# Ten-stage transformer kernel: stage ends with y weighed before its root, x ended by one operation, squares of x by halves, one weight split on GpSimd, modulation between Rwkv's turns

## What is computed

```python
x = x + 0.5 * rmsnorm(swiglu(rmsnorm(x, ng[0]), ...), ng[1])        # feed-forward
h = rmsnorm_2(x, norm_w[i, 0]) * (1.0 + sc1) + sh1                  # mixers of the second block
y = short_conv_mixer(h, ...)
x = x + gt1 * rmsnorm_2(y, norm_w[i, 1])
def rmsnorm(x, g, eps=NORM_EPS):
    y = xf * lax.rsqrt(jnp.mean(xf * xf, -1, keepdims=True) + eps)
    return y * g
```

## Time and profile before

| | us |
|---|---|
| three runs | 3035.13, 3039.06, 3039.35 |
| profiled execution | 3035.5 |
| its span | 3033.6 |
| TensorE matmuls busy | 2805.1 (92%) |
| VectorE busy | 1293.2 (43%) |
| ScalarE busy | 1121.9 (37%) |
| GpSimd busy | 162.3 (5%) |
| mean granted TensorE clock | 0.962 |
| read from HBM | 697.5 MB, 230 GB/s over the span |

### The profile page before, as it was taken

One profiled execution on the slowest core, in us unless ns is written; L12 is line 12 of the kernel. 1 busy time (PEld: TensorE's weight loads), 2 busy tenths in 40 slices (PEclk: granted clock), 3 DMA queues, 4 the chain that ended last, 5 costly groups with the idle time before them and its releaser, 6 DMA issues.

```text
span 3033.6 us, 44027 instructions
## 1 busy us (share of the span) xinstructions
PE 2805.1 (92%) x18364; PEld 2211.1 (73%) x18364; DVE 1293.2 (43%) x2125; ACT 1121.9 (37%) x2008; POOL 162.3 (5%) x146
## 2 busy tenths in 40 slices
PE   8989879999989999799899999999896879999998
PEld 6879657887878888578797666666695856666665
DVE  5546267546557544364563121212474551121212
ACT  5444245435457222254443222222454251222222
POOL 0000000000000222100010000000003300000000
PEclk9999899999999999799999999999897989999999
DMA  8524657436434111065244899999550036999996
GB/s 338 184 104 167 250 224 303 181 139 236 181 139 168 42 56 56 28 234 193 107 174 174 361 415 415 417 414 416 217 180 1 1 125 276 417 415 416 413 418 252
DMA packets 96401, 701.53 MB, mean 231 GB/s; under 512 B 10688, under 2 KB 10816, under 8 KB 11328
## 3 DMA queue, kind: packets, MB, share of 16 engines
q1 hardware_dynamic: 96192, 698.59, 58.0%
HBM read 697.50 MB, written 1.05 MB: 230 GB/s over the span
## 4 chain that ended last, share of the span: by engine, by line
PE 86%; DVE 6%; ACT 4%; issue 2%; DMA 1%; POOL 1%; SPq 0%; DVEq 0%; ACTq 0%
PE bank L1576 15%; PE bank L811 11%; PE bank L813 11%; PE bank L812 11%; PE bank L1636 8%; PE bank L1554 4%; PE bank L1663 4%; PE bank L1914 2%; PE bank L1922 2%; PE bank L1926 2%; DMA weight_ring<-weight_slots 1%; DVE h_sb L716 1%; PE bank L2429 1%; PE bank L1445 1%; PE bank L1448 1%
## 5 line engine op out<-in xcount | busy, mean ns | idle before, releaser
L1576 PE MATMUL bank<-weight_ring,packed_h 128*64 128x256 f32 x2176 | 285.4, 379 | 0.0
L811 PE MATMUL bank<-source_hi_lo,weight_hi_lo 128*128 128x256 f32 x864 | 252.3, 292 | 14.8 <-DVE source_hi_lo L801 11.7
L1576 PE MATMUL bank<-more_slots,packed_h 128*64 128x256 f32 x1920 | 257.0, 379 | 1.5 <-ACT packed_h L1563 1.5
L811 PE MATMUL bank<-gate_up_hi_lo,x_hi_lo 128*128 128x512 f32 x640 | 253.4, 396 | 1.4 <-DVE gate_up_hi_lo L929 1.4
L1576 PEld LDWEIGHTS bank<-weight_ring,packed_h 128*64 128x64 f32 x2176 | 196.6, 137 | 74.0 <-issue 18.1
L813 PE MATMUL bank<-gate_up_hi_lo,x_hi_lo 128*128 128x512 f32 x640 | 249.8, 390 | 0.0
L812 PE MATMUL bank<-gate_up_hi_lo,x_hi_lo 128*128 128x512 f32 x640 | 249.2, 389 | 0.0
L812 PE MATMUL bank<-source_hi_lo,weight_hi_lo 128*128 128x256 f32 x864 | 249.0, 288 | 0.0
L813 PE MATMUL bank<-source_hi_lo,weight_hi_lo 128*128 128x256 f32 x864 | 248.7, 288 | 0.0
L1576 PEld LDWEIGHTS bank<-more_slots,packed_h 128*64 128x64 f32 x1920 | 174.3, 137 | 69.4 <-issue 15.4
L770 DVE TENSOR_TENSOR weight_hi_lo<-weight_ring,weight_hi_lo 128x1024 fp32r<-128x1024 f32 x138 | 168.2, 1221 | 100.6 <-ACT weight_hi_lo L764 100.6
(11 more groups left out here) (548 smaller groups left out, 5409.6 us busy)
## 6 DMA issues: line engine op xcount, KB each, us to landing
weight_ring<-weight_slots SPq DMA_DIRECT2D x443, 1024.0 KB, 7.4
more_slots<-weight_slots SPq DMA_DIRECT2D x212, 1024.0 KB, 9.0
params_sb<-small_params SPq DMA_DIRECT2D x1, 3196.5 KB, 17.7
h_sb<-weight_slots SPq DMA_DIRECT2D x3, 1024.0 KB, 5.8
y_sb<-weight_slots SPq DMA_DIRECT2D x3, 1024.0 KB, 7.9
x_sb<-x_by_tokens SPq DMA_DIRECT2D x1, 1024.0 KB, 4.8
out_by_tokens<-x_sb SPq DMA_DIRECT2D x4, 256.0 KB, 2.2
params_sb<-small_params SPq DMA_DIRECT2D x1, 69.5 KB, 4.6
```

The costliest lines, as they stand in the source:

```text
L811: e.matmul(out, w[0], x[0], start=start, stop=False, skip_group_check=shared)
L1576: mm = e.matmul(ps[x * CAP:(x + 1) * CAP, m * FB:(m + 1) * FB], self.hc[:, c, (2 * (p % 2) + x) * CAP:(2 * (p % 2) + x + 1) * CAP], wt[:, ...
```

## The change

1. In `back_dve` VectorE multiplies y by the gain row (`out_weighed`) as soon as a bank's square is made, ahead of the reciprocal. One operation then ends x: y_tok times the inverse root, plus x.
2. Of x's norm, the squares of q=1 are made in halves of 512 features, each as soon as its half of x is new; VectorE turns the first sum into a bias (`x_part`). VectorE scales all of x, four operations of 512 columns; ScalarE scales none. The head of VectorE comes wholly behind the stage's last operation on x.
3. In NsaSsd, Conv and Delta GpSimd makes the low part of split 0 alone; split 1 is made by ScalarE and VectorE behind the sources. A slot is free when both its units' low parts are made (`done` with two signals).
4. In Rwkv the first of the four modulation steps stands between the turns of q=0 and q=1 on TensorE, and VectorE makes the low part of split 0 behind `norm_dve`'s first part.

```diff
@@ head_act
-        for q in range(TT):
-            self.squares_act(e, q)
-            e.wait_ge(*k.ge("x_inverse", n, q))
-            e.activation(k.h_tok[:, q, 0:512], k.x[:, q, 0:512], ACT.Copy, scale=k.x_inv[:, q:q + 1])
-            if q == 0:
-                self.begin(e)
-                self.first_split_act(e)
+        self.squares_act(e, 0)
+        for f in range(2):
+            cut = slice(f * 512, f * 512 + 512)
+            e.wait_ge(*k.ge(*self.x_key(1, f)))
+            e.activation(k.y_tok[:, 1, cut], k.x[:, 1, cut], ACT.Square, accum_out=k.x_sums[:, 1 + f:2 + f])
+        e.wait_ge(*k.ge("x_half_squared", n, 1))
+        e.wait_ge(*k.ge("x_part", n))
+        e.activation(k.x_dev[:, 1:2], k.x_sums[:, 2:3], ACT.Sqrt, scale=1.0 / D, bias=k.x_part[:, 0:1])
+        self.begin(e)
+        self.first_split_act(e)
@@ head_dve
-        self.scaled_dve_half(e, 1)
+        self.inverse_of_x_dve(e, 0)
+        self.scale_x_dve(e, 0, 0)
+        e.wait_ge(*k.ge("x_half_squared", n, 0))
+        e.tensor_scalar(k.x_part[:, 0:1], k.x_sums[:, 1:2], 1.0 / D, NORM_EPS, ALU.mult, ALU.add)
+        self.scale_x_dve(e, 0, 1)
+        self.inverse_of_x_dve(e, 1)
+        for f in range(2):
+            self.scale_x_dve(e, 1, f)
@@ back_dve
         for q in range(TT):
-            e.wait_ge(*k.ge("out_squared", n, 2 * q))
-            e.tensor_scalar(k.y_part[:, q:q + 1], ...)
+            for f in range(2):
+                b, cut = 2 * q + f, slice(f * 512, f * 512 + 512)
+                if q == 0:
+                    e.wait_ge(*gain_in(f))
+                e.wait_ge(*k.ge("out_squared", n, b))
+                if f == 0:
+                    e.tensor_scalar(k.y_part[:, q:q + 1], ...)
+                e.tensor_tensor(k.y_tok[:, q, cut], k.bank[b][:, :], self.gain_row[:, cut], ALU.mult)
             e.wait_ge(*k.ge("out_deviation", n, q))
             e.reciprocal(k.y_inv[:, q:q + 1], k.y_dev[:, q:q + 1])
             e.wait_ge(*k.ge("out_inverse", n, q))
             for f in range(2):
-                e.scalar_tensor_tensor(out=k.y_tok[:, q, cut], in0=k.bank[2 * q + f][:, :], scalar=k.y_inv[:, q:q + 1], in1=self.gain_row[:, cut], ...)
-            if nxt and q:
-                nxt.first_half_dve(e)
-            for f in range(2):
-                e.tensor_tensor(k.x[:, q, cut], k.x[:, q, cut], k.y_tok[:, q, cut], ALU.add)
+                e.scalar_tensor_tensor(out=k.x[:, q, cut], in0=k.y_tok[:, q, cut], scalar=k.y_inv[:, q:q + 1], in1=k.x[:, q, cut],
+                                       op0=ALU.mult, op1=ALU.add)
@@ plan_units
-            k.weights.done(i, self.lo_key(u))
+            k.weights.done(i, self.lo_key(u), self.lo_key(u - 1))
@@ Conv, NsaSsd, Delta
-        self.plan_units(12, column_half, 2)
+        self.plan_units(12, column_half, 1)
-        self.norm_act(e, ..., lambda: self.split_act(e, 1))
+        self.norm_act(e, ...)
+        self.split_act(e, 1)
         self.norm_dve(e, ...)
+        self.split_dve(e, 1)
-        self.split_pool(e, 1)
@@ Rwkv
-        self.norm_pe(e)
-        k.modulation.fill(e, "PE", 4)
+        self.norm_pe(e, lambda: k.modulation.fill(e, "PE", 1))
+        k.modulation.fill(e, "PE", 3)
-        self.split_dve(e, 0)
-        self.norm_dve(e, k.par("a1_gain2"), None, lambda c: self.first_mix_dve(e, c))
+        self.norm_dve(e, k.par("a1_gain2"), None, lambda c: self.first_mix_dve(e, c), lambda: self.split_dve(e, 0))
```

More of the change, by code:

```diff
@@ L538, in x_T, with turn_in_pe @@
         return self.k.bank[(6, 7, 0, 1)[2 * q + c // 4]][:, c % 4 * P:c % 4 * P + P]
-    def turn_in_pe(self, e, src, came, read):
+    def turn_in_pe(self, e, src, came, read, between=None):
         k, n = self.k, self.n
@@ L552, in turn_in_pe @@
                     mm.then_inc(*k.up("in_turned", n, q, c // 4))
+            if q == 0 and between:
+                between()
     def squares_act(self, e, q):
@@ L646, in norm_act, with norm_dve @@
                 behind(c)
-    def norm_dve(self, e, gain, shift=None, behind=None):
+    def norm_dve(self, e, gain, shift=None, behind=None, between=None):
         k, n = self.k, self.n
@@ L656, in norm_dve @@
                     e.tensor_scalar(k.h[:, c, q * P:(q + 1) * P], self.x_T(q, c), gain[:, c:c + 1], shift[:, c:c + 1], ALU.mult, ALU.add).then_inc(*k.up(*self.h_key(c, q)))
+        if between:
+            between()
         if behind:
@@ L706, in back_dve @@
         for q in range(TT):
-            e.wait_ge(*k.ge("out_squared", n, 2 * q))
-            e.tensor_scalar(k.y_part[:, q:q + 1], k.y_sums[:, 2 * q:2 * q + 1], s2 / D, s2 * NORM_EPS, ALU.mult, ALU.add).then_inc(*k.up("out_part", n, q))
+            for f in range(2):
[3 more added lines that the diff above has]
+                e.wait_ge(*k.ge("out_squared", n, b))
+                if f == 0:
+                    e.tensor_scalar(k.y_part[:, q:q + 1], k.y_sums[:, b:b + 1], s2 / D, s2 * NORM_EPS, ALU.mult, ALU.add).then_inc(*k.up("out_part", n, q))
+                e.tensor_tensor(k.y_tok[:, q, cut], k.bank[b][:, :], self.gain_row[:, cut], ALU.mult).then_inc(*k.up("out_weighed", n, q, f))
             e.wait_ge(*k.ge("out_deviation", n, q))
@@ L3611, in act @@
         self.x_r = self.x_r_in
-        self.norm_act(e, k.gain[:, 1, 0, :], k.mod[1][:, 0:C], lambda c: self.source_hi(e, "h", k.h, c, self.h_key(c)), lambda: self.split_act(e, 1))
+        self.norm_act(e, k.gain[:, 1, 0, :], k.mod[1][:, 0:C], lambda c: self.source_hi(e, "h", k.h, c, self.h_key(c)))
+        self.split_act(e, 1)
         self.inputs_act(e)
```

47 lines of the change are left out of this document (21 added, 26 removed).

## The result

The changed kernel took **3013.59 us** (median of 4 runs, 3010.85 to 3018.26) against 3037.82 us of the kernel before (median of 4, 3035.13 to 3039.35): ratio 0.9923, 95% interval 0.9906 to 0.994. That is 24.2 us less where about 20 had been forecast (3019.0 against 3039.06), and inside the range of 3011 to 3027. The profiled execution is the slowest of the four: 3018.26 us, span 3016.4, which is 17.2 us under the span of before, where 18.4 had been forecast. So two numbers have to be explained: what the seams gave, and why the median gained more than the profiled execution.

What follows compares the result with a forecast made beforehand. TensorE paces the kernel, so time saved at its nine seams and the end stays saved. 10.2 + 4.2 + 0.45 + 2.2 + 1.3 = 18.4 us less gives 3017.1 or 3020.7, middle 3019.0; range 3011 to 3027 (8 in 10).

Steps and rivals of the forecast that it cites:

- Prices (a) to (d): New operations: y's weighing 0.70 us, x's one operation 0.75, half square about 0.70, VectorE's scaled copy 0.49.
- Rival 1: x's last operation is slow, 0.53 us more each, 21 us over ten seams, result 3038.4; chance 3%.
- The seam: First seam: x whole 1.85 us earlier, turns end at 212.65 instead of 214.73, worth 2.1 us.
- another 0.5 us in the squares would cost nothing: First seam, x's norm: TensorE's turns now bound it, so squares 0.5 us longer would lose nothing.
- VectorE stood until GpSimd was done: First source_lo took 1.58 us, held by GpSimd's second split; moving that split saves 1.2 us at three seams.
- The Rwkv term: Seam into Rwkv: source_lo starts at 896.6 instead of 897.03, 0.45 us gained.
- these end at 893.2, as late as before, although they start 0.45 earlier: Rwkv seam: turns end no earlier because modulation's first step, 1.9 us at the low level, stands between them.
- TensorE itself would be done 1.0 us earlier: Rwkv seam: TensorE finishes its modulation 1.0 us earlier but waits for the sources.
- The feed-forward seams and the end: Into feed-forward stages 2.2 us together: 1.0 between two such, 0.6 behind each of two mixers; program end 1.3.
- Rival 2: The gain stops at the next queue, VectorE or ScalarE late: 12.6 us gained, 3023 to 3026; chance 15%.
- wait behind unit 0 for the moved split: NsaSsd, Conv, Delta: split has 1.7 us to spare at the low level; at the high level a 0.5 wait.
- Rival 3: The clock rises earlier behind three deep seams, 2.2 us each, 6.7 in all, 3010 to 3014; chance 8%.

Runs made afterwards that it cites:

- run 3: The changed kernel with x q=1 squared whole instead of by halves; 3013.07 us, ratio 0.9935 to the kernel before.
- Run 4: The changed kernel with the second weight split back on GpSimd in NsaSsd, Conv and Delta; 3018.87 us, ratio 0.9951 to the kernel before.
- run 5: The kernel before with only the second weight split of NsaSsd, Conv and Delta moved off GpSimd, behind VectorE's source_lo; 3031.74 us, ratio 0.9984.
- Run 1: The kernel before with only the new end of y and x (weighing early, one operation ends x); 3026.97 us, ratio 0.9971.
- run 2: The changed kernel with y scaled twice, then added to x, as before; 3025.32 us, ratio 0.9969 to the kernel before.
- run 7: The changed kernel with both Rwkv edits undone: modulation step behind all turns, VectorE's split ahead of its norm; 3013.46 us, ratio 0.9927 to the kernel before.
- run 6: The changed kernel with only Rwkv's first modulation step put back behind all sixteen turns; 3011.39 us, ratio 0.9917 to the kernel before.
- second profile: Profiled execution of the unaltered changed kernel when measured once more; span 3009.6 us, mean granted clock 0.968.
- run 8: The changed kernel once more, unaltered, beside the kernel before; 3012.63 us, ratio 0.9923.

## Why the prediction was right, and where it was not

**What bounds the kernel: right.** The mixture stages kept their rows to the digit, and the end of the program came by what the seams gave.

**Prices (a) to (d): right**, 0.68, 0.749, 0.76 and 0.49 for what was taken as 0.70, 0.75, 0.70 and 0.49; the third is a half square (0.63) with its accumulator read, from its start at 208.32 to the next step at 209.08. **Rival 1, with the skill's rule, is refuted:** the Trainium skill, Vector Engine (DVE) Microarchitecture Reference, section "Points that are easy to get wrong", would have halved the rate of x's operation; 40 rows with both tensors in SBUF in fp32 take 0.744 to 0.753, as the form with one tensor in a bank does. (This rival's price, 21 less 18.4, is 2.6 and not the 2.9 written there, which changes nothing.)

**The seam: right step by step**, each within 0.15 us, and "another 0.5 us in the squares would cost nothing" is run 3. "VectorE stood until GpSimd was done", 1.2 us, is runs 4 and 5 (1.27 and 1.17). The step on which the sum rests and which the prediction never said is that its parts need each other. Run 1 gave 7.9 us by seams and run 2 8.5, 16.4 together where the whole gave 19.9; at the first seam the parts gave 0.33 and 1.86 apart and 3.23 together.

**The Rwkv term was mis-sized**: 0.45 forecast, 1.36 measured. What failed is "these end at 893.2, as late as before, although they start 0.45 earlier". It took the low level for all of the second turns. They were done 9.81 us after the last product instead of 10.84, because the clock rose within them (1.31 for eight, not 1.98). Run 4 shows the other case, since its Rwkv stage is that of the changed kernel and the clock stayed low there up to 889.9:

```profile
884.49 1.94 PE bank L551 x8
886.43 1.86 PE bank L2034 x16
888.29 1.82 PE bank L551 x8
```

These turns are done at 10.73 and the last source_lo at 18.87 us, 0.43 earlier than before: the forecast's 0.45. So the term was right for the low level, and that the level rose in time was luck of 0.9 us. The term also read the kernel before wrongly. There the chain did not go from VectorE's split to VectorE's norm, but by a small operation behind the split to ScalarE, as in run 7:

```profile
892.18 0.09 DVE one_less_mu L2291
...
892.30 1.14 ACT h_sb L637 x4
```

And the part about "TensorE itself would be done 1.0 us earlier" overlooked what run 6 showed: without the step between them the turns are done at 8.32 and VectorE's chain ends 1.5 earlier. The chain there waits for the turns, which have no pause any more, so work put between them costs most of its own length (1.5 of 1.86 in run 6).

**The feed-forward seams and the end** were 0.47 and 0.43 too small. Behind the two mixers the prediction counted ScalarE's root alone. It came 0.58 us earlier, as forecast (0.6), but in the kernel before it wasn't what the first product waited for: that came right behind the turns of q=1, and in the changed kernel it comes behind ScalarE's weight splits and its part of x. The chains of before and after:

```profile
499.77 1.97 PE bank L550 x8
```

```profile
498.10 1.03 ACT x_hi_lo L974 x4
```

So the seam shrank from what the turns set to what ScalarE sets, 0.96 and 0.72. At the end the second bank's square is ready in time, so both weighings run back to back: x q=0 is whole 2.87 us after out_part, against 4.11 before. At the first seam the second weighing waits for its square until 203.30, and the reciprocal, free at 203.52 by the root, comes at 203.91.

**Rival 2 came in part.** The change lost 2.7 us between seams in its first profile, most of it in NsaSsd (280.4 us for 277.9); no queue of the seam did that, and in the second profile the stage took 275.3, so this is scatter and not a price of the change. One piece is a transfer. In the chain of waits from 320 to 376 us TensorE had run up to 8 us ahead of before and then stood for it:

```profile
338.25 12.36 DMA weight_ring<-weight_slots
```

Before, the same wait was 4.75 us. Here what TensorE had won ahead of this point, beyond what the transfers had won, was given back. In the second profile the wait is as long (12.10), but TensorE is 6.4 us ahead a few products behind it, where the first was 2.7 ahead; why the transfer came earlier there is not shown. The other piece is the clock (run 8). And "wait behind unit 0 for the moved split" never showed at the low level, 0.4 us of it in the second profile and 0.8 with the clock up: the prediction's 1.7 to spare, and its 0.5 without.

**Rival 3 came in part too**: behind NsaSsd's seam the level came back earlier in the second profile, 1.7 us. That such pieces make the median's 24 from the seams' 20 is argued. The clocks on record fit it: 51 executions of the kernel before, timed beside the runs, have a mean granted clock of 0.958 to 0.964, the eight of the changed kernel 0.963 to 0.968. But where the low stretches fell is seen in one profile of the kernel before alone, and why they are fewer stays open. So of the median's 24.2 us the seams explain 19.9, and the other 4.3 are not explained.

## What to carry to other kernels

When two engines hand a seam to each other, cost the parts of a change together: one that shortens VectorE's chain is worth 0.33 us while ScalarE's queue holds the next step, and 1.37 once that queue is short. Ask of each moved operation at which clock level TensorE will be: a split that hides behind unit 0 at the low level became a wait of 0.4 to 0.8 us at the high one, and keeping the clock up was worth only what the other engines left.

## What the runs showed that had not been expected

- Filling TensorE's idle places with products held the granted clock at 1.00 over all nine seams of the changed kernel, and sped eight turns from 1.97 to 1.04 us, but the kernel by only 4 us of 3012.6.
- The whole gain of the change at the first seam, 3.23 us, is the same in two executions whose spans differ by 6.8 us (3016.4 at 0.963 and 3009.6 at 0.968): seam by seam such a change can be read more finely than from totals that scatter by several. Where the clock rises within a seam it moves too: with the same order NsaSsd's was 10.03 to 10.42 us over four profiles, and Rwkv's 17.82 to 18.87 over three.
- VectorE's scaled copy out of and into SBUF is held by GpSimd as well as source_lo is: 1.05 us at 211.98 beside GpSimd's first split in the kernel before, and 1.04 to 1.05 at the two other seams with a GpSimd split, against 0.49 in its nine other places; 0.48 in the changed kernel, where it ends as GpSimd starts. Out of a bank, VectorE's norm keeps its 0.34 beside GpSimd.
